# Moving the 24 chunks of the adaLN modulation product from VectorE sums to TensorE products

## The reference, cut to what matters

```python
cond = jax.nn.silu(c)                                   # (1, 1024)
for i in range(DEPTH):                                  # 2 layers
    mod = (cond @ mod_w[i] + mod_b[i]).reshape(B, 6, D_MODEL)   # mod_w[i]: (1024, 6144)
    h = modulate(rmsnorm(x, g[0]), mod[:, 0], mod[:, 1])
    y = diff_attention(h, ...)                          # layer 1: mlstm_layer
    x = x + mod[:, 2][:, None, :] * rmsnorm(y, g[1])
    h = modulate(rmsnorm(x, g[2]), mod[:, 3], mod[:, 4])
    y = swiglu(h, ...)                                  # layer 1: moe_swiglu
    x = x + mod[:, 5][:, None, :] * rmsnorm(y, g[3])
```

## Time and profile before

| | |
|---|---|
| three executions | 2169.73, 2170.09, 2179.38 us (median 2170.09) |
| span of the profiled execution, from its first to its last instruction | 2170.9 us |
| TensorE matmul records busy | 1724.5 us, 79% of the span |
| VectorE busy | 474.3 us, 22% |
| ScalarE busy | 185.4 us, 9% |
| DMA | 484.72 MB, 223 GB/s in the mean |
| chain that ended last | PE 70%, issue 10%, DMA 8%, DVE 7% |

### The profile page before, as it was taken

How to read it: one execution, slowest core, us unless ns; L and a number is a source line. 1 busy time by engine, 2 the same in 40 slices (tenths; PEclk the granted TensorE clock), 3 DMA queues, 4 the chain that set the end, 5 groups by cost and what they waited for, 6 DMA issues and landing times.

```text
span 2170.9 us, 18533 instructions
## 1 busy us (share of the span) xinstructions
PE 1724.5 (79%) x7558; PEld 1060.3 (49%) x7559; DVE 474.3 (22%) x1045; ACT 185.4 (9%) x404; POOL 33.2 (2%) x70
## 2 busy tenths in 40 slices
PE   0496799998978886687999968699996848768486
PEld 0374388844746633326996323299632313232232
DVE  0677235401563413101000000100001000100101
ACT  0104100001102101100000001000001001010010
POOL 0000000000020000000000000000000000000000
PEclk9997899999999887898999989999997979979798
DMA  9593239673401043397645429966651997969886
GB/s 300 179 379 140 78 144 342 218 283 117 155 1 39 0 160 111 140 402 278 220 166 198 152 82 336 396 238 227 237 195 55 396 368 268 402 243 399 324 309 252
DMA packets 219137, 484.72 MB, mean 223 GB/s; under 512 B 17545, under 2 KB 20002, under 8 KB 218914
## 3 DMA queue, kind: packets, MB, share of 16 engines
q1 hardware_dynamic: 205090, 481.46, 59.9%
q10 hardware_dynamic: 13824, 0.47, 0.4%
HBM read 480.86 MB, written 1.05 MB: 222 GB/s over the span
## 4 chain that ended last, share of the span: by engine, by line
PE 70%; issue 10%; DMA 8%; DVE 7%; ACTq 2%; ACT 1%; SPq 1%; POOL 0%; DVEq 0%; POOLq 0%
PE ps L786 15%; PE ps L1084 13%; PE ps L1054 13%; PE ps L1103 9%; DMA ring<-in_moe_w_down 7%; PE ps L773 6%; PE ps L1028 2%; PE ps L1131 2%; PE ps L815 1%; DMA ring<-in_moe_w_up 1%; DVE arena L1171 1%; ACTq L553 1%; PE ps L1063 1%; DVE hT L1205 1%; SPq L399 1%
## 5 line engine op out<-in xcount | busy, mean ns | idle before, releaser
L1054 PE MATMUL ps<-ring,arena 128*64 128x512 f32 x672 | 318.0, 631 | 47.9 <-issue 47.5
L1103 PE MATMUL ps<-ring,arena 128*64 128x512 f32 (+3 forms) x1120 | 322.6, 597 | 30.7 <-DMA ring<-in_moe_w_down 30.7
L786 PE MATMUL ps<-hT,ring 128*128 128x256 f32 x1472 | 327.3, 384 | 9.3 <-DVE hT L1205 7.6
L1055 PE MATMUL ps<-ring,arena 128*64 128x512 f32 x672 | 318.4, 631 | 0.0
L786 PEld LDWEIGHTS ps<-hT,ring 128*128 128x128 f32 x1472 | 281.4, 192 | 51.9 <-DVE hT L1205 8.8
L1084 PE MATMUL ps<-arena,ring 128*128 128x208 f32 (+1 forms) x1792 | 291.5, 326 | 0.0
L1084 PEld LDWEIGHTS ps<-arena,ring 128*128 128x128 f32 x1792 | 291.2, 190 | 0.0
L1103 PEld LDWEIGHTS ps<-ring,arena 128*64 128x64 f32 (+3 forms) x1120 | 110.2, 147 | 233.1 <-issue 179.5
L1054 PEld LDWEIGHTS ps<-ring,arena 128*64 128x64 f32 x672 | 94.1, 144 | 236.1 <-issue 234.3
L1028 PE MATMUL ps<-arena 128*128 128x128 f32 (+2 forms) x256 | 51.3, 384 | 151.1 <-issue 151.1
L773 PE MATMUL ps<-ring,arena 128*128 128x512 f32 x368 | 161.4, 601 | 1.5 <-DVE arena L1338 1.5
(11 more groups left out here) (262 smaller groups left out, 872.5 us busy)
## 6 DMA issues: line engine op xcount, KB each, us to landing
ring<-in_moe_w_gate SPq DMA_DIRECT2D x56, 2048.0 KB, 20.3
ring<-in_moe_w_up SPq DMA_DIRECT2D x56, 2048.0 KB, 18.8
ring<-in_moe_w_down SPq DMA_DIRECT2D x56, 2048.0 KB, 21.3
ring<-in_mod_w SPq DMA_DIRECT2D x24, 2048.0 KB, 11.9
ring<-in_mlstm_w_in SPq DMA_DIRECT2D x8, 2048.0 KB, 8.5
ring<-in_attn_w_in SPq DMA_DIRECT2D x6, 2048.0 KB, 10.5
ring<-in_ffn_w_gate SPq DMA_DIRECT2D x5, 2048.0 KB, 12.9
ring<-in_ffn_w_up SPq DMA_DIRECT2D x5, 2048.0 KB, 12.3
```

Of the source, the lines that this page charges most:

```text
L786: ins = pe.matmul(dst, w[:, k, c * P:(c + 1) * P], hT[:, k, :], start=(k == 0), stop=(k == KT - 1))
L1054: pe.matmul(ps[0:width, b], x_k, wg[:, k, :], start=(k == 0), stop=(k == KT - 1))
L1055: ins = pe.matmul(ps[low, b + 1], x_k, wu[:, k, :], start=(k == 0), stop=(k == KT - 1))
L1103: ins = pe.matmul(ps[r, 4 + 2 * st + n], eh[:, ft, st * P:st * P + sw[st]], w[:, k, n * 512:(n + 1) * 512], start=(ft == 0), stop=(ft == E ...
```

## The change

The products of all 24 chunks go to TensorE. `cond` becomes 128 x 8 x 63, zero but for column 31, so that a window of 32 columns has the conditioning column at place j. TensorE reads the chunk in the ring itself: 8 blocks by 4 strips, 32 matmuls a chunk in place of 4, accumulating over the blocks. VectorE's `mod_chunk`, the buffer's use and the semaphore `acc_ready` are gone; a slot with a modulation chunk is free when `mod_summed` says that TensorE has read it. GpSimd clears `cond` early, and ScalarE waits for GpSimd's constants before it writes column 31.

```diff
-    mod = lambda layer, j: (f"mod{layer}", j * WC, WC, "dve")
+    mod = lambda layer, j: (f"mod{layer}", j * WC, WC, "pe")
...
-        cond = sb("cond", [P, KT])
+        cond = sb("cond", [P, KT, 63])
...
-            if r == "dve":
+            if m.startswith("mod"):
                 n_mod += 1
-                read_by.append((acc_ready, n_mod))
+                read_by.append((mod_summed, n_mod))
...
+            pool.memset(cond[:, :, 0:31], 0.0)
+            pool.memset(cond[:, :, 32:63], 0.0)
...
-            act.activation(cond[:], c_cols, ACT.Silu).then_inc(cond_ready, 1)
+            act.wait_ge(consts, 1)
+            act.activation(cond[:, :, 31], c_cols, ACT.Silu).then_inc(cond_ready, 1)
...
-            def mod_sum(layer, j, n):
-
-                pe.wait_ge(acc_ready, n + 1)
-
-                for i in range(4):
-                    r = slice(32 * i, 32 * (i + 1))
-                    ins = pe.matmul(ps[r, 7, 0:P], ones_col[:, 31 - j:63 - j], mod_acc[:, n % 2, i * P:(i + 1) * P],
-                                    start=(j in MOD_PARTS[layer]), stop=(j + 1 in MOD_PARTS[layer]))
+            def mod_product(layer, j):
+
+                i = chunk(f"mod{layer}", j * WC)
+                w = slot_up(i % SLOTS)
+                for k in range(KT):
+                    for q in range(4):
+                        ins = pe.matmul(ps[32 * q:32 * (q + 1), 7, 0:P], cond[:, k, 31 - j:63 - j], w[:, k, q * P:(q + 1) * P],
+                                        start=(k == 0 and j in MOD_PARTS[layer]),
+                                        stop=(k == KT - 1 and j + 1 in MOD_PARTS[layer]))
                 ins.then_inc(mod_summed, 1)
...
+            pe.wait_ge(cond_ready, 1)
             for j in range(4):
-                mod_sum(0, j, mods)
-                mods += 1
+                mod_product(0, j)
...
-            dve.wait_ge(cond_ready, 1)
-            mods = 0
-            for j in range(4):
-                mod_chunk(0, j, mods)
-                mods += 1
-
             modulation(1, 0, 4)
...
-                for m in MODS[0][j]:
-                    mod_chunk(0, m, mods)
-                    mods += 1
...
-                for m in MODS[1][j]:
-                    mod_chunk(1, m, mods)
-                    mods += 1
...
+    nc = bacc.Bacc("TRN2", target_bir_lowering=False, num_devices=1, dynamic_dma_scratch_size=1024)
```

More of the change, by code:

```diff
@@ L210, in trunk @@
         junk = lambda i: xn[:, i // 2, (i % 2) * 512:(i % 2 + 1) * 512]
-        mod_acc = area(1024).rearrange("p (b n) -> p b n", b=2)
+        area(1024)
         mod_rows = area(P)
@@ L282, in trunk @@
         cond_ready = sem("cond_ready")
-        acc_ready = sem("acc_ready")
         mod_summed = sem("mod_summed")
@@ L818, in pe_program @@
                     for m in MODS[0][j - 1]:
-                        mod_sum(0, m, mods)
-                        mods += 1
+                        mod_product(0, m)
             mod_turn(2)
@@ L878, in pe_program @@
                     if j and c < len(MODS[1][j - 1]):
-                        mod_sum(1, MODS[1][j - 1][c], mods)
-                        mods += 1
+                        mod_product(1, MODS[1][j - 1][c])
             mod_turn(3)
@@ L1159, in full @@
                 return ps[:, (n - 1) % UB]
[L1161 to L1175, removed]
             def modulation(n, first, last):
@@ L1667 @@
     from concourse.bass_utils import run_bass_kernel_spmd
-    nc = bacc.Bacc("TRN2", target_bir_lowering=False, num_devices=1)
+    nc = bacc.Bacc("TRN2", target_bir_lowering=False, num_devices=1, dynamic_dma_scratch_size=1024)
     arrays, args = {}, {}
```

## The result

The changed kernel takes 2202.28 us (median of four executions, 2199.78 to 2203.6), beside 2171.86 us (2169.73 to 2179.38) for the kernel before on the same chip. The ratio is 1.0129, 95% interval 1.0108 to 1.0151: 1.3% slower. The forecast was 2196 us, 1.2% slower.

A forecast was written before the change was run, and what follows sets the result against it. Mostly TensorE bounds the kernel, but its start is bound by ScalarE's queue and four vector sums in series. Terms -2.6, +12.1 and +16.0 give +25.5 us on the 2170.9 span: 2196 us, likeliest 2187 to 2209, range 2181 to 2230.

The forecast's parts named there:

- Start: Up to the input projection's first product: vector sums leave the path, ScalarE's queue takes most back; first product 86.8, -2.6 us.
- The step with the most weight in it: At the start: early-freed slots keep q1 busy to 75.6 us, so ScalarE is released at 74.9, 21.6 us later.
- Input projection: Three pairs and two singles of products cost more than sums on TensorE, no load late: +12.1 us.
- an allowance: Slow clock at the input projection's start, 0 to 3 us, counted in the likeliest case's range.
- SwiGLU: Dense SwiGLU: eleven of twelve single products cost 1.54 us each, the wait for `up` falls to 0.8: +16.0 us.
- Behind it: Everything after the dense SwiGLU: unchanged in order and only shifted, 0 us.
- 27 ns a record: Price of a product's matmul records, four strips side by side; a single product costs 1.54 us more than a sum.
- Rival 2: Long product runs don't keep 27 ns: 2230 us at 55 ns, about 2300 at 0.11 us a record; chance 0.17.
- Rival 1: Start: the queue doesn't hold ScalarE, 24.3 us gained, sum +3.8, 2174 us; chance 0.13 with what lies up to the forecast.
- Rival 3: Faster, under 2165 us: early-free slots relieve a later load wait, with the start's 24 us and cheap products; chance 0.04.

The follow-up runs named there:

- a_ring_held: Changed kernel, but SyncE issues the eighth ring load only after ScalarE has passed its small loads and first activation behind them: 2180.85 us, ratio 1.0023.
- a_strip_by_strip: Changed kernel with a product's block and strip loops exchanged, eight matmuls in a row to one strip: 2281.41 us, ratio 1.0479.
- a_half_width: Changed kernel with blocks 1 to 7 of each chunk multiplied over 64 of 128 columns, comparable only ahead of the router: 2176.17 us, ratio 0.9997.
- a_loads_late: Changed kernel with ScalarE's seven small loads issued behind its work on `x`: 2158.0 us, ratio 0.9916.
- b_loads_late: Kernel before, with the vector sums, and ScalarE's seven small loads issued behind its work on `x`: 2138.6 us, ratio 0.9836.

## Why the prediction was right, point by point

- **Start, forecast -2.6 us, measured -0.5** (first product 88.98; 89.44 before). The step with the most weight in it, that the queue holds ScalarE for 21.6 us longer, came out at 21.3 (74.59; forecast 74.9), and a_ring_held shows the cause by undoing it alone. That it came out to 0.3 us is in part luck. The sum takes the release to come when q10 has passed 10970 packets, read from the kernel before with the packets of 52 to 54 us spread evenly; but 3334 of these 4161 passed in the first 1.26 us, so the count at the old release was 11683, and with it the same sum gives about 75.9. In the changed kernel the release came at 10924 packets. So the count at which an issue is let go isn't fixed; this step is off by a us at most, and the mechanism stands. Four ring loads without a gap and a dry queue at 75.8 (forecast 75.6) are as written. What the term missed is the last small issue, L559, which took 2.75 us (0.60 in the kernel before and in a_ring_held). The ring's queue had just run dry at that time; why q10 then went more slowly than in the kernel before (1668 packets from 75.8 to 77 us, 1390 a us, where 3334 from 52 to 53.26 us are 2650 a us) stays open. The copy stood at 81.65 in place of 79.9.
- **Input projection, forecast +12.1, measured +13.7** (copy to copy less the start: 189.17 less 175.94 is 13.2, and 0.5 were gained at the start). Three pairs cost 3.06 us more each (3.63 and 0.57 in the chains), the single 1.53, the last one 1.3; that is 12.0. The other 1.7 us are the clock at the first 128 records, which the forecast had as an allowance and not in the sum.
- **SwiGLU, forecast +16.0, measured +15.3** (from its first product to the copy of bank 7: 285.85 to 466.88, and 272.99 to 438.75). Eleven products at 1.53 are 16.8; the wait for `up` fell from 1.69 to 0.86 (forecast 0.8), and the first 160 records took 0.4 us less. The twelfth product is hidden, as forecast.
- **Behind it, forecast 0, measured +1.0** (29.1 at the end less the 28.1 at the copy). The broadcast of the gate (L762) got 1.6 us back, since it ran at the faster clock: 1.89 us in place of 3.48, with a granted clock of 1.00 from 467 to 469 us, and 0.50 from 440 to 442 us in the kernel before. At the router the kernel was 25.5 us behind the one before, at the end 29.1. Those 3.6 us come in the experts' branches in pieces I can't put down to one cause, so they stay open; the long idle pieces at the branches are alike in both (10.80 and 10.75, 25.96 and 25.99).
- **27 ns a record** was the price called least sure. 64 records take 1.89 us in place of 4 x 0.44, and a_strip_by_strip and a_half_width show both what it is (columns of four strips at once) and what it isn't (issue). The first four products, at half that pace, are the exception, and lie off the path. Rival 2 is out. (Its 0.11 us a record would have cost 19 x 5.3 = 101 us, not 105.)
- **Rival 1** was not what happened, but a_ring_held is the kernel in which it does: 2180.85 us beside a kernel before of 2176.37, ratio 1.0023, where the forecast for the rival was +3.8 us.
- **Rival 3**, faster, needed the start's gain and cheap products together. a_loads_late is that kernel, and its 2158.0 us (ratio 0.9916) are indeed under 2165. But b_loads_late takes 2138.6 us, so even then the sums are the better choice.

The forecast's 2196 is 3.6 us short on the span's account of 25.5 against 29.1: 2.1 at the start, 1.6 in the projection (the clock), 1.0 behind the SwiGLU, less 0.7 in it and 0.4 between the projection and it. The medians are 30.4 us apart, 1.3 more than the spans, and the kernel before is now at 2171.86 in place of 2170.09; both are within the spread of its executions.

The version that beats both is the kernel before with its small loads issued later: 1.6% faster, with nothing else changed. With the first four chunks as products besides (h_first_four_loads_late) it is the same, 1.6%.

## What to carry to other kernels

Work that is moved off an engine with spare time, onto the one that is busy without a gap, costs its full length there; what it frees counts only where somebody waited for it. Ask of each buffer that comes free earlier which queue its next load will share, and who sits behind the issue of small loads in the other queue: here 22 us of gain were lost to seven loads that only layer 1 needs, and moving them was worth more than the change. And when two versions differ by a per cent around runtime branches, look at the idle times at the branches before explaining the difference by the edit: 52 instructions that nothing waits for moved the time by 20 to 27 us here.

## What the runs showed of the hardware

- A queue of 16 to 32 byte elements beside a queue of 2048 byte ones passes as many packets as that one (1728 and 1726 in 10 us), and an engine's next issue is held until most of the earlier packets have passed: 34.12 us in one instruction of ScalarE, let go when 10924 of the queue's 13824 packets had passed (11683 in the kernel before).
- Four strips of 32 array columns run side by side when consecutive matmuls alternate among them: 27 ns a record of 128 columns, 92 ns when eight in a row stay in one strip.
- With the wait of 2.6 us in front of a long run of matmuls filled, the clock was at 2.4 GHz from their start (27.79 us for 128 records); behind idle waits of 2.6 to 3.2 us they took 29.30 to 30.94 us in nine kernels, but 27.89 in the kernel before. Why that one was at the full pace behind the same kind of wait is open; its TensorE had short bursts of sums every 6 us up to 82 us.
- 52 more instructions of TensorE, of matmuls that nothing waits for, cost 20 to 27 us, nearly all of it in idle time at the branches behind them; 256 more cost nothing.
